# Down projections as seven block products of sums, and half of the weight sums by an accumulating transfer

## What is computed

```python
def swiglu_ffn(x, g, w_gu, w_down):
    h = rmsnorm(x, g) @ w_gu
    a, b = jnp.split(h, 2, axis=-1)
    return (jax.nn.silu(a) * b) @ w_down
```

## Time and profile before

| | |
|---|---|
| median of 3 runs | 1809.26 us (1804.97 to 1809.34) |
| profiled execution | 1808.28 us, span 1806.5 us |
| TensorE busy | 1741.4 us, 96% |
| VectorE, ScalarE, GpSimd busy | 1151.8, 885.1, 348.6 us |
| DMA engines, share of the 16 | q1 45.8%, mean 152 GB/s |

### The profile page before, as it was taken

The page is one execution under the profiler, slowest core; times in us unless marked ns, Lnnn a source line. Parts: engine busy times, 40 slices in busy tenths (PEclk is TensorE's granted clock), DMA queues, the critical chain, the costliest instruction groups (busy, mean ns, idle before and its releaser), DMA issues. The chain is left out here.

```text
span 1806.5 us, 41781 instructions
## 1 busy us (share of the span) xinstructions
PE 1741.4 (96%) x16593; PEld 1616.2 (89%) x16593; DVE 1151.8 (64%) x2113; ACT 885.1 (49%) x1579; POOL 348.6 (19%) x261
## 2 busy tenths in 40 slices
PE   8999999999999999999998999999989999999998
PEld 7999998889999999999997677776769999999998
DVE  4766775579828828555653466666656994595481
ACT  5355445465525524455632455555555653354252
POOL 3333332000120130333531011112200004003012
PEclk9999999899999999999999999999999999999999
DMA  5333222323423332342356999999983334234232
GB/s 129 85 108 85 83 84 66 87 79 94 118 71 94 95 94 71 87 147 62 117 172 205 384 374 379 385 385 367 366 287 99 94 94 117 61 97 115 57 100 70
DMA packets 291541, 273.79 MB, mean 152 GB/s; under 512 B 22034, under 2 KB 252531, under 8 KB 290836
## 3 DMA queue, kind: packets, MB, share of 16 engines
q1 hardware_dynamic: 289412, 268.63, 45.8%
q10 hardware_dynamic: 1792, 1.44, 0.3%
q0 software_dynamic: 144, 1.05, 0.2%
HBM read 254.64 MB, written 16.43 MB: 150 GB/s over the span
## 5 line engine op out<-in xcount | busy, mean ns | idle before, releaser
L2117 PE MATMUL ps<-xh,f_l 128*128 128x288 f32 x1232 | 279.2, 298 | 0.2 <-DVE f_l L2373 0.2
L2137 PE MATMUL ps<-f_h,f_l 128*128 128x288 f32 x1748 | 243.0, 296 | 0.2 <-DVE t_small L2482 0.2
L2137 PEld LDWEIGHTS ps<-f_h,f_l 128*128 128x128 f32 x1748 | 236.1, 189 | 0.4 <-DVE t_small L2482 0.4
L2117 PEld LDWEIGHTS ps<-xh,f_l 128*128 128x128 f32 x1232 | 208.6, 189 | 0.6 <-DVE f_l L2373 0.5
L2117 PE MATMUL ps<-xl,f_l 128*128 128x288 f32 x704 | 208.3, 296 | 0.0
L2117 PE MATMUL ps<-f_l 128*128 128x288 f32 x1056 | 156.8, 297 | 7.6 <-ACT t_small L2264 4.2
L2447 DVE TENSOR_TENSOR xT<-xT,ps 128x576 f32<-128x576 f32 x48 | 36.2, 754 | 197.1 <-PE ps L2137 197.1
L1586 DVE COPY at_kt<-ps 128x512 f32<-128x512 f32 x128 | 88.2, 691 | 109.7 <-PE ps L1289 109.2
L2117 PEld LDWEIGHTS ps<-f_l 128*128 128x128 f32 x1056 | 146.2, 189 | 9.0 <-ACT t_small L2264 5.0
L2117 PEld LDWEIGHTS ps<-xl,f_l 128*128 128x128 f32 x704 | 133.6, 190 | 0.0
L653 POOL TENSOR_TENSOR a_wl<-a_wraw,a_wh 128x1024 fp32r<-128x1024 f32 x32 | 78.5, 2456 | 200.6 <-ACT a_wh L548 185.4
(11 more groups left out here) (434 smaller groups left out, 4064.4 us busy)
## 6 DMA issues: line engine op xcount, KB each, us to landing
xT<-in_cache_k SPq DMA_DIRECT2D x40, 512.0 KB, 6.1
xT<-in_cache_v SPq DMA_DIRECT2D x40, 512.0 KB, 6.6
a_wraw<-in_a_w_in SPq DMA_DIRECT2D x32, 512.0 KB, 4.2
f_h_plain<-in_cache_k SPq DMA_DIRECT2D x30, 512.0 KB, 6.4
xl_plain<-in_cache_v SPq DMA_DIRECT2D x30, 512.0 KB, 6.5
f_h_plain<-in_cache_v SPq DMA_DIRECT2D x30, 512.0 KB, 7.0
xl_plain<-in_cache_k SPq DMA_DIRECT2D x29, 512.0 KB, 6.3
a_wraw<-in_w_gate_up SPq DMA_DIRECT2D x44, 256.0 KB, 4.1
```

The source lines that it names most:

```text
L2117: mm = pe.matmul(place(m, pos), wt[:, at], combination(2 * q, part, b), start=pos in (0, 1, 3) and t == 0 and i == 0, stop=t == len(pairs) ...
L2137: mm = pe.matmul(ps[:, first + a, 0:HALF], wt[:, at], hidden(i, part)[:, a * HALF:(a + 1) * HALF], start=opens and t == 0 and y == 0, stop ...
```

## The change

- **Down units as gate units.** They take the same `PRODUCTS`: seven positions x p pairs x 3 matmuls. The hidden tiles therefore are kept as seven combinations too: `cross` makes them on VectorE from the two products, one more operation for an even tile, three dependent ones for an odd tile, and `round_hidden` and `low_hidden` work on one group for an even tile (2 x 288 columns) and two for an odd one (3 x 288 and 2 x 288).
- **Residual.** `residual` takes six reads of the banks for each down unit: after positions 0, 1, 2, 4 and 6 of 288 columns each, after 5 of 576. TensorE's positions 2, 4, 5 and 6 wait for them.
- **Chunks** are 3, 3, 3 and 2 pairs instead of 4, 4 and 3, so there are 16 down units in a trunk instead of 12. Slots are six instead of seven.
- **Low parts** of down blocks are made by VectorE, no longer by GpSimd.
- **Sums by transfer.** From the third fast unit on, in all gate units and in the down units of three pairs, SyncE loads five blocks (A21 twice, at S1 and at S3), and GpSimd then issues one accumulating transfer in SBUF that adds A22 to S1 and A11 to S3. VectorE makes only S2 and S4, in its positions 4 and 6. The last chunk's down units and the first two gate units keep all four folds.
- **Last chunk.** Its first down unit follows its last gate unit; TensorE does the first pair of position 3 ahead of position 2.
- **Trunk 0's second weight unit after the block** waits on GpSimd for the last product.
- **Attention.** The prompt's units start at steps 9, 16, 24, 32, 40, 48, 56 and 64 instead of 15, 22, ... 64; the first rounding of queries moves from step 9 to 4, a small copy from 2 to 4.

```diff
-    FIRST_UNIT, PAIR_STEPS, PARTS_AT, OUT_AT, TAIL_AT = 15, 7, 4, 5, 6
+    PARTS_AT, OUT_AT, TAIL_AT = 4, 5, 6
+    FIRST_UNIT, LAST_UNIT = 9, KSTEPS
+    STARTS = [FIRST_UNIT + j * (LAST_UNIT - FIRST_UNIT) // (KD - 1) for j in range(KD)]
...
-    chunks = [(0, 8), (8, 16), (16, KF)]
+    chunks = [(0, 6), (6, 12), (12, 18), (18, KF)]
...
-    SLOTS, AHEAD, LEAD, HRING = 7, 5, 4, 9
+    SLOTS, AHEAD, LEAD, HPAIRS = 6, 5, 4, 3
...
+    def by_transfer(m):
+        n = KD + m
+        return m >= 2 and (kind(n) == "g" or UNITS[n][1] < C - 1)
...
-                    wanted = ((A22, 1, 1), (S3, 1, 0), (A11, 0, 0), (A12, 0, 1)) if kind(n) == "g" else ((A11, 0, 0), (A12, 0, 1), (S1, 1, 0), (A22, 1, 1))
+                    wanted = [(A22, 1, 1), (S3, 1, 0), (A11, 0, 0), (A12, 0, 1)]
+                    if by_transfer(m):
+                        wanted = [(A22, 1, 1), (A11, 0, 0), (S1, 1, 0), (S3, 1, 0), (A12, 0, 1)]
...
-                    if kind(KD + m) == "g":
-                        if which in FOLDS:
-                            act.wait_ge(e["folded"], 4 * gates_before(m) - 3 + FOLDS.index(which))
+                    if by_transfer(m) and which in (S1, S3):
+                        act.wait_ge(summed_up[m % 2], transfers(m))
+                    elif which in FOLDS:
+                        act.wait_ge(e["folded"], fold_at[m, which] + 1)
...
                 def round_hidden(i):
-                    act.wait_ge(e["product"], i + 1)
-                    if i >= HRING:
-                        act.wait_ge(e["multiplied"], base[unit_at["d", chunk_of[i - HRING], ROWS - 1] - KD + 1])
-                    act.activation(halves(hidden(i, 0)), entered(i), ACT.Copy).then_inc(e["hhigh"], 1)
+                    act.wait_ge(e["hcrossed"], crossings(i) + (3 if i % 2 else 1))
+                    if i // 2 >= HPAIRS:
+                        act.wait_ge(e["multiplied"], base[unit_at["d", chunk_of[i] - 1, ROWS - 1] - KD + 1])
+                    for g in groups(i):
+                        act.activation(hidden_group(i, 0, g), source(g), ACT.Copy).then_inc(e["hhigh"], 1)
...
+                def add_operands(n):
+
+                    m = n - KD
+                    pool.wait_ge(fetched[m % 2], fetches(m))
+                    pool.dma_start(operand(m, S1, 2), operand(m, A22, 2), accum_op=ALU.add).then_inc(summed_up[m % 2], 16)
...
+                    if by_transfer(m):
+                        dve.wait_ge(summed_up[m % 2], transfers(m))
+                        if which == S4:
+                            dve.wait_ge(e["folded"], fold_at[m, S2] + 1)
+                    elif which != S1:
+                        dve.wait_ge(e["folded"], fold_at[m, S1 if which in (S2, S3) else S2] + 1)
...
                 def low_hidden(i):
-                    dve.wait_ge(e["hhigh"], i + 1)
-                    dve.tensor_tensor(halves(hidden(i, 1)), entered(i), halves(hidden(i, 0)).bitcast(F32), ALU.subtract).then_inc(e["hlow"], 1)
+                    for which, g in enumerate(groups(i)):
+                        dve.wait_ge(e["hhigh"], combined(i) + which + 1)
+                        dve.tensor_tensor(hidden_group(i, 1, g), source(g), hidden_group(i, 0, g).bitcast(F32), ALU.subtract).then_inc(e["hlow"], 1)
...
+                def residual(n, pos):
+
+                    m, (_, c, j) = n - KD, UNITS[n]
+                    low, high = (halves(k.xT[:, 2 * j + a, :]) for a in range(2))
+                    x, op = {0: (low[:, 0, :], ALU.subtract), 1: (high[:, 1, :], ALU.add), 2: (low[:, 1, :], ALU.subtract),
+                             4: (high[:, 1, :], ALU.add), 5: (low, ALU.subtract), 6: (high[:, 0, :], ALU.add)}[pos]
...
                             if pos == 0 and mixed(n) is not None:
                                 multiply(mixed(n), n - 1 - KD)
+                                cross(mixed(n), e["product"], e["hcrossed"])
                             if kind(n) == "d":
...
+                                if pos in (0, 1, 2, 4, 5):
+                                    residual(n, pos)
```

More of the change, by code:

```diff
@@ L1091, in out_step, with unit_at @@
         return mixed_last[c] + 1
+    def unit_at(n):
+        j = sum(start <= n for start in STARTS) - 1
+        return j, n - STARTS[max(j, 0)]
     def unit_pair(n):
-        j, i = divmod(n - FIRST_UNIT, PAIR_STEPS)
-        return 4 * j + i if 0 <= j < KD and i < 4 else None
+        j, i = unit_at(n)
+        return 4 * j + i if j >= 0 and i < 4 else None
     ring, ordinal = {}, {"act": {}, "dve": {}}
@@ L1857, in pairs_of @@
         return list(range(first // 2, end // 2))
-    def out_banks(n, tile):
-        if tile == 1 and kind(n + 1) == "g":
-            return 4
-        return DOWN_BANKS[tile][(n - KD) % 2]
     def mixed(n):
@@ L1873, in trunk @@
         if kind(n) == "d":
-            for tile in sorted(range(2), key=lambda x: closing(n, x)):
-                take[m, closing(n, tile)] = len(take)
+            for pos in (0, 1, 2, 4, 5, 6):
+                take[m, pos] = len(take)
             continue
@@ L2114, in product @@
                             pe.wait_ge(e["comblow"], combined(2 * q) + (1 if b < 2 else 2 if b >= 4 else 3))
+                        if kind(n) == "d" and UNITS[n][2] == 0:
+                            pe.wait_ge(e["hlow"], combined(2 * q) + (1 if b < 2 else 2 if b >= 4 else 3))
                         at = slice(t * P, (t + 1) * P)
                         for i, (wt, part) in enumerate(((high, 0), (high, 1), (low, 0))):
-                            mm = pe.matmul(place(m, pos), wt[:, at], combination(2 * q, part, b), start=pos in (0, 1, 3) and t == 0 and i == 0,
+                            right = combination(2 * q, part, b) if kind(n) == "g" else hidden(q, part, b)
+                            mm = pe.matmul(place(m, pos), wt[:, at], right, start=pos in (0, 1, 3) and t == 0 and i == 0,
@@ L2118, in product @@
                                            stop=t == len(pairs) - 1 and i == 2, skip_group_check=True)
[L2119 removed]
+                    if some.stop is None:
                         mm.then_inc(e["multiplied"], 1)
[L2122 to L2139 removed]
@@ L2297, in _ @@
                     elif n in fast:
-                        for pos in range(steps(n)):
+                        for pos in range(SPAN):
                             if kind(n) == "g" and pos < 3:
@@ L2347, in _ @@
                     if n in fast:
-                        if kind(n) == "d":
-                            for pos in range(4):
-                                low_block(n, pos)
+                        if by_transfer(n - KD):
+                            add_operands(n)
                         continue
```

237 lines of the change are left out of this document (107 added, 130 removed).

## The result

| | before | after |
|---|---|---|
| median | 1809.15 us (1804.97 to 1809.34) | 1884.56 us (1880.52 to 1885.88) |
| profiled execution, span | 1808.28, 1806.5 us | 1885.88, 1884.1 us |
| TensorE busy, matmuls | 1741.4 us, 16,593 | 1736.9 us, 16,329 |
| VectorE, ScalarE, GpSimd busy | 1151.8, 885.1, 348.6 us | 1345.9, 947.2, 295.9 us |
| granted clock, mean | 0.991 | 0.982 |

The change makes the kernel slower, by a ratio of 1.0421 (1.0404 to 1.0437), 75 us. The forecast was 1840, its range ended at 1874. The sign was right, the size was not.

What follows compares the result with a forecast made beforehand. The prediction took TensorE to bound both feed-forward stages and full DMA engines the attention. Fewer matmuls, -35.2 us, against +26, +9, +11.6, +7.5 and +11.7 of waits summed to +30.6 on about 1809: 1840, range 1812 to 1874.

Runs made afterwards that it cites:

- e8: The changed kernel with its 64 accumulating transfers turned into plain copies of the same bytes, same issuer and place, so outputs differ; 1846.41 us in one execution.

## What to carry to other kernels

A transfer that takes an engine's work has two prices: its length from the last load to the sum, and what stands behind the first instruction that waits for it. Work out the second for every place where the transfer is used, with the landing of the last load and not of the first; two gate units in each chunk cost 37 of the transfers' 41 us here. And before an engine's share is read as room, read it over the repeating unit alone: 80 of 89 us was 21.5 of 22.4.

## What the runs showed of the hardware

- An accumulating transfer within SBUF takes longer the larger it is: 3.0, 3.3, 4.5 and 4.9 us for 192, 256 (one block), 384 and 512 KB (two blocks), where a plain copy by the same engine takes 2.8 to 3.2 for 384 and 512 KB. While one ran, the DMA engines were at 0.91 to 0.92 of their time at some 150 GB/s; during a plain copy in e8 at 0.62 and 199 GB/s.
- GpSimd's issue of an accumulating transfer took 0.85 to 1.2 us, that of a plain copy 0.53 to 0.73.
- A VectorE operation on two SBUF operands that starts beside a GpSimd addition of 1.3 us ends only with it, 1.01 and 1.44 us for 0.45.
- Spacing of matmuls in a full queue is the same before and after, 0.133 us where the granted clock is 1.
- Of the six waits of 2.4 to 3.7 us at the ends of the chunks four were followed by matmuls at the lower granted clock, those of 2.40 and 3.16 us were not; one of 1.90 us was.
